# One fused kernel of a mixed transformer block: two in-order queues of the paired attention loop are re-ordered, and the multiplies of the MLA up-projection move from GpSimd to VectorE

## The chip, the cores and the metric

The kernel runs on one core of one Trainium2 chip. The metric is the device time of one execution in microseconds (us). It was run three times; the middle value counts. A core has TensorE (PE; its weight loads are listed as PEld), VectorE (DVE), ScalarE (ACT), GpSimd (POOL) and SyncE (SP), each with an in-order queue of its own, joined by semaphores. Work goes through SBUF (tiles named AR, RW, RX, RA) and the eight banks of PSUM (PS).

## The reference, cut to what matters

The reference is a first block (modulation, recurrent mixer, dilated attention) and two further blocks with mixture-of-experts layers. The first of the two, the "even" layer, has a differential attention and a grouped-query attention. The second, the "odd" layer, is a latent attention (MLA) with 16 heads, 512 queries and 768 keys:

```python
def mla_project(h, w_in, q_norm, w_q_up, kv_norm, w_kv_up, qk_norm):
    cq, ckv, kr = jnp.split(h @ w_in, [MLA_Q_RANK, MLA_Q_RANK + MLA_KV_RANK], axis=-1)
    q = (rmsnorm(cq, q_norm) @ w_q_up).reshape(bsz, t, MLA_HEADS, MLA_NOPE + MLA_ROPE)
    kv = (rmsnorm(ckv, kv_norm) @ w_kv_up).reshape(bsz, t, MLA_HEADS, MLA_NOPE + MLA_VDIM)
    qn = rmsnorm(q[..., :MLA_NOPE], qk_norm[0, :MLA_NOPE])
    qr = rmsnorm(q[..., MLA_NOPE:], qk_norm[0, MLA_NOPE:])
    kn = rmsnorm(kv[..., :MLA_NOPE], qk_norm[1, :MLA_NOPE])
    ...
def mla_attend(qn, qr, kn, kr, v, scale):
    s = jnp.einsum('bqhd,bkhd->bhqk', qn, kn) + jnp.einsum('bqhr,bkr->bhqk', qr, kr)
    p = jax.nn.softmax(s.astype(jnp.float32) * scale, axis=-1).astype(v.dtype)
    return jnp.einsum('bhqk,bkhd->bqhd', p, v)
```

## The kernel before

Everything is float32. Each engine's queue is written out by one function per stage, and every engine runs its stages in the same order.

**Paired attention.** Two stages use the `..._pairs` functions: the grouped-query attention of the even layer (ATB, 48 units) and the MLA attention of the odd layer (ATO, 64 units). A unit is 128 queries of one head against 768 keys (256 in the last 16 units of ATB). The loop is a software pipeline over steps. In step s TensorE computes the scores of unit s (line 655) into banks 0 and 1 or 2 and 3, then the fill items of this step, then the transposes of the probabilities of unit s-2 (line 666, into banks 4 and 5; for odd units one more transpose, line 670, of the reciprocal sums), and in even steps the product with the values for units s-4 and s-3 together (line 866, "pv", into bank 6). VectorE takes the maximum of the scores (line 755), a reciprocal (906), copies the transposed probabilities of even units out of PSUM (916), and scales the product out of bank 6 (924, "the scaling"). ScalarE does the exponential (710, two records: the activation and the reading of its sum) and the copy of the odd units (890). GpSimd spreads the reciprocals (834).

**Fill items.** A unit can carry extra work, done four steps later by each engine, as `fill(it)`. In ATO these are the up-projections of the next four heads ("group"): 13 items i = 0 to 12 for each of three groups, one a step; item i stands in step 18+i for the second of them (first item in an even step), item 12 is the last. Group 1 has its items 0 to 2 together in step 4, and then one a step. The very first group is projected ahead of the loop, alone (the "prologue"). A group has ten tiles k, six of key and value (k = 0 to 5) and four of query (k = 6 to 9). Item i does on TensorE the transposes of tile i-3 (line 2500, "ut", into bank 6) and then the projection of tile i (2518 for a key tile, 2511 for a query tile, "up", into bank 7). On ScalarE it copies tile i-3 out of bank 6 (2528), copies tile i out of bank 7 and squares it (2539 and 2540, or 2536 and 2537), and does Ln and Exp (2548, 2550) for the norm of tile i-1, after VectorE's part for it. On VectorE it sums the squares of tile i-1 (2561, 2563, 2565, 2568) and finishes and applies the norm of tile i-2 (2580 to 2588, 2591). On GpSimd it copies parts of tile i-1 (2602, 2606) and multiplies tile i-2 by gain and rotary tables (2617 to 2629), after which the semaphore `upU` lets TensorE transpose it.

A bank is filled again only when its reader is done: "pv" and "ut" share bank 6, so an ut waits for the scaling of the product before it, and a product waits for ScalarE's 2528; "up" of item i+1 waits for ScalarE's square of item i. In ATB the 13 fill items are a square on ScalarE (1785) and a sum on VectorE (1793) for each of six tiles, one norm, and six multiplies (1803), in steps 4 to 16.

The weights of the experts of the odd layer are loaded only after the last product of ATO (`Q.wait_ge("full", "pv", "o", 63)`), and the loads behind ATB wait for its last product in the same way.

Of the kernel before, what the change touches and what calls it, by code (L numbers as in the profile page):

```python
# [6 lines left out]
ALU = mybir.AluOpType  # L7
# [127 lines left out]
class Banks:  # L135
# [5 lines left out]
    def fill(self, b, *label):  # L141
        n = self.n.get(b, 0)
        if n and self.e.seen.get(f"read{b}", 0) < n:
            self.e.e.wait_ge(self.c.sem(f"read{b}"), n)
            self.e.seen[f"read{b}"] = n
        self.n[b] = n + 1
        self.c.bank[label] = (b, n + 1)
        return b
# [5 lines left out]
def program(nc, T, out, known):  # L154
    ctx = ExitStack()
    with ctx:
# [19 lines left out]
        def bank(b):  # L176
            return PS[:, b, :]
# [700 lines left out]
        def act_pairs(A, fill=None):  # L878
            n = len(A.units)
            for step in range(n + 4):  # L880
                i = step - 4
                if 0 <= i < n:
                    for it in A.fill[i]:
                        fill(it)
                i = step - 2
                if i % 2 and 0 <= i < n:
                    nk = A.units[i]["nk"] + 128
                    pt_free(S, A, i)
                    S.wait_ge("full", "tr", A.tag, i)
                    s.copy(A.Pt[i % len(A.Pt)][:, 0:nk], psf[:, 2048:2048 + nk]).then_inc(*S.read("tr", A.tag, i))  # L890
                if step < n:
                    act_exp(A, step)

        def dve_pairs(A, fill=None):
            n = len(A.units)
            for step in range(n + 4):
                if step < n:
                    dve_max(A, step)
                i = step - 1
                if i % 2 and 0 <= i < n:  # L900
                    a = (i - 1) % 8
                    V.wait_ge("read", "sc", A.tag, i - 1)
                    V.wait_ge("read", "sc", A.tag, i)
                    if i >= 8:
                        V.wait_ge("rb", A.tag, i - 8)
                    v.reciprocal(A.rd[:, a:a + 2], A.den[:, a:a + 2]).then_inc(*V.up("rd", A.tag, i))
                i = step - 4
                if 0 <= i < n:
                    for it in A.fill[i]:
                        fill(it)  # L910
                i = step - 2
                if i % 2 == 0 and 0 <= i < n:
                    nk = A.units[i]["nk"]
                    pt_free(V, A, i)
                    V.wait_ge("full", "tr", A.tag, i)
                    v.tensor_copy(A.Pt[i % len(A.Pt)][:, 0:nk], psf[:, 2048:2048 + nk])\
                        .then_inc(*V.read("tr", A.tag, i))
                i = step - 3
                if i % 2 and 0 <= i < n:
                    b = V.bank_of(("pv", A.tag, i))  # L920
                    nk = A.units[i]["nk"]
                    V.wait_ge("read", "tr", A.tag, i)
                    V.wait_ge("full", "pv", A.tag, i)
                    v.tensor_tensor(A.units[i]["out"], bank(b)[:, 0:128], A.Pt[i % len(A.Pt)][:, nk:nk + 128], ALU.mult)\
                        .then_inc(*V.read("pv", A.tag, i))


        OUTP = {"oute": 6, "outo": 4}
# [1624 lines left out]
        def dve_up(gi, i):  # L2553
            if 0 <= i - 1 < 10:
                k = i - 1
                isq = UP[k][1]
                A_, U_, W_, q_ = STM[(10 * gi + k) % 3]
                n_, hw_ = (8, 96) if isq else (4, 64)
                Sv = U_[:, 0:4 * hw_].rearrange("p (h f) -> p h f", h=4)
                V.wait_ge("read", "up", gi, k)  # L2560
                v.tensor_reduce(q_[:, 0:4], Sv[:, :, 0:64], AX, ALU.add).then_inc(*V.up("upr", gi, k))
                if isq:
                    v.tensor_reduce(q_[:, 4:8], Sv[:, :, 64:96], AX, ALU.add).then_inc(*V.up("upw"))
                    V.wait_ge("upw")
                    v.tensor_scalar(q_[:, 4:8], q_[:, 4:8], 2.0, None, ALU.mult).then_inc(*V.up("upw"))
                    V.wait_ge("upw")
                V.wait_ge("upr", gi, k)
                v.tensor_scalar(q_[:, 8:8 + n_], q_[:, 0:n_], 1.0 / 64, EPS, ALU.mult, ALU.add)\
                    .then_inc(*V.up("upa", gi, k))
            if 0 <= i - 2 < 10:  # L2570
                k = i - 2
                j, isq = UP[k]
                A_, U_, W_, q_ = STM[(10 * gi + k) % 3]
                n_ = 8 if isq else 4
                a_, y_, z_ = q_[:, 8:8 + n_], q_[:, 8 + n_:8 + 2 * n_], q_[:, 0:n_]
                Av = (A_[:, 0:384] if isq else A_).rearrange("p (h f) -> p h f", h=4)
                Uv = U_.rearrange("p (h f) -> p h f", h=4)
                Wv = W_.rearrange("p (h f) -> p h f", h=4)
                V.wait_ge("upy", gi, k)
                v.tensor_tensor(z_, y_, y_, ALU.mult).then_inc(*V.up("upw"))  # L2580
                V.wait_ge("upw")
                v.tensor_tensor(z_, z_, a_, ALU.mult).then_inc(*V.up("upw"))
                V.wait_ge("upw")
                v.tensor_scalar(z_, z_, -0.5, 1.5, ALU.mult, ALU.add).then_inc(*V.up("upw"))
                V.wait_ge("upw")
                v.tensor_tensor(y_, y_, z_, ALU.mult).then_inc(*V.up("upw"))
                V.wait_ge("upw")
                v.tensor_tensor(Av[:, :, 0:64], Av[:, :, 0:64], y_[:, 0:4].unsqueeze(2).broadcast_to([128, 4, 64]),
                                ALU.mult).then_inc(*V.up("upn", gi, k))
                if isq:  # L2590
                    v.tensor_tensor(Av[:, :, 64:96], Av[:, :, 64:96],
                                    y_[:, 4:8].unsqueeze(2).broadcast_to([128, 4, 32]), ALU.mult)\
                        .then_inc(*V.up("upw", gi, k))

        def pool_up(gi, i):
            k = i - 1
            if 0 <= k < 10 and not UP[k][1]:
                j = UP[k][0]
                A_, U_, W_, q_ = STM[(10 * gi + k) % 3]
                grp_free(G, gi)  # L2600
                G.wait_ge("read", "up", gi, k)
                g.tensor_copy(GRP[gi % 2][2][:, j, :].rearrange("p (h f) -> p h f", h=4),
                              A_.rearrange("p (h f) -> p h f", h=4)[:, :, 64:128]).then_inc(*G.up("upv", gi, j))
                G.wait_ge("kr", 5)
                G.wait_ge("upr", gi, k)
                g.tensor_copy(U_.rearrange("p (h f) -> p h f", h=4)[:, :, 64:96],
                              krn[:, j, :].unsqueeze(1).broadcast_to([128, 4, 32])).then_inc(*G.up("upk", gi, k))
            k = i - 2
            if 0 <= k < 10:
                j, isq = UP[k]  # L2610
                A_, U_, W_, q_ = STM[(10 * gi + k) % 3]
                Av = (A_[:, 0:384] if isq else A_).rearrange("p (h f) -> p h f", h=4)
                Uv = U_.rearrange("p (h f) -> p h f", h=4)
                Wv = W_.rearrange("p (h f) -> p h f", h=4)
                gg = gm[:, 0:64] if isq else gm[:, 96:160]
                G.wait_ge("upn", gi, k)
                t = g.tensor_tensor(Uv[:, :, 0:64], Av[:, :, 0:64], gg.unsqueeze(1).broadcast_to([128, 4, 64]), ALU.mult)
                if isq:
                    G.wait_ge("upw", gi, k)
                    g.tensor_tensor(Uv[:, :, 64:96], Av[:, :, 64:96],  # L2620
                                    TM[:, 0, j, 0, :].unsqueeze(1).broadcast_to([128, 4, 32]), ALU.mult)
                    for q4 in range(4):
                        p4 = q4 ^ 1
                        t = g.tensor_tensor(Wv[:, :, 8 * q4:8 * q4 + 8], Av[:, :, 64 + 8 * p4:72 + 8 * p4],
                                            TM[:, 0, j, 1, 8 * q4:8 * q4 + 8].unsqueeze(1).broadcast_to([128, 4, 8]),
                                            ALU.mult)
                    t.then_inc(*G.up("upr4", gi, k))
                    G.wait_ge("upr4", gi, k)
                    t = g.tensor_tensor(Uv[:, :, 64:96], Uv[:, :, 64:96], Wv, ALU.add)
                t.then_inc(*G.up("upU", gi, k))  # L2630

        OT4 = AR[:, XN0:XN0 + 4096].rearrange("p (c t) -> p c t", c=8)
        units, fills = [], {}
# [233 lines left out]
```

## Time and profile before

| what | value |
|---|---|
| time, median of 3 runs | 2594.24 us (2591.68 to 2594.48) |
| the profiled execution | 2594.48 us |
| its span in the trace | 2593.2 us |
| busy in the span | PE 2268.0 us (87%), PEld 1280.5 (49%), DVE 1288.5 (50%), ACT 985.4 (38%), POOL 463.1 (18%) |
| ATB, paired part | about 745 to 857 us |
| up-projection ahead of ATO (prologue) | about 1681 to 1721 us |
| ATO | about 1721 to 1977 us |

Times in rows are microseconds from the start of the span unless marked ns. PE busy is a modelled figure, since matmuls are pipelined; a granted clock (PEclk) of 1.00 is 2.4 GHz and 0.50 is 1.2 GHz.

### The profile page before, as it was taken

The page shows a single profiled execution, that of the slowest core. Times are in us where ns is not written, and L with a number is a line of the kernel's source. Part 1 is how long each engine was busy: PE and PEld are TensorE (multiplying, and loading weights), DVE is VectorE, ACT ScalarE, POOL GpSimd, SP SyncE. Part 2 cuts the span into 40 slices and gives each one's busy share as a digit, 9 for nine tenths or more (in the row PEclk, how much of TensorE's full clock was granted, in tenths as well). Part 3 has the DMA queues.
Part 4 walks back from the last instruction along what each step waited for, and adds up shares of the span by engine and source line. Part 5 has one row for each costly group of instructions (what it writes and reads, how often), then busy time and mean ns, then how long its engine had stood idle before and what let it go on. Part 6 is the DMA issues. An engine that isn't in the chain of part 4 may idle for free.

```text
span 2593.2 us, 26567 instructions
## 1 busy us (share of the span) xinstructions
PE 2268.0 (87%) x10249; PEld 1280.5 (49%) x10249; DVE 1288.5 (50%) x2295; ACT 985.4 (38%) x1612; POOL 463.1 (18%) x463
## 2 busy tenths in 40 slices
PE   5998988999989995999999997779999887777776
PEld 2443534445657453667666674436665432222222
DVE  2137524625875226898889985456662421111111
ACT  2015333213554124888888884245552100000000
POOL 0000000000111111354456620032321000000000
PEclk8999989999999997999999998889999889999999
DMA  7111511011000337899999998300014689999998
GB/s 271 65 65 66 197 63 69 33 49 66 1 1 1 131 155 276 334 370 367 381 372 370 369 364 297 125 1 1 1 66 163 252 316 404 403 401 403 404 412 342
DMA packets 92428, 546.32 MB, mean 211 GB/s; under 512 B 7791, under 2 KB 10623, under 8 KB 67598
## 3 DMA queue, kind: packets, MB, share of 16 engines
q1 hardware_dynamic: 81886, 518.95, 51.0%
q0 software_dynamic: 6144, 20.98, 3.6%
q10 hardware_dynamic: 4272, 4.69, 0.5%
q8 instruction: 82, 1.34, 0.2%
q14 instruction: 44, 0.36, 0.0%
HBM read 523.62 MB, written 20.97 MB: 210 GB/s over the span
## 4 chain that ended last, share of the span: by engine, by line
PE 53%; DMA 17%; DVE 16%; ACT 7%; issue 5%; POOL 1%; SPq 0%; ACTq 0%; DVEq 0%; POOLq 0%
DMA AR<-in_w_exp_gate_dram 13%; PE PS L655 7%; PE PS L1650 7%; DVE RW L1996 7%; PE PS L953 5%; PE PS L2030 5%; PE PS L2215 4%; PE PS L666 3%; PE PS L866 3%; ACT AR L2084 3%; PE PS L1340 3%; ACT RW L1988 2%; PE PS L1174 2%; PE PS L415 2%; PE PS L690 2%
## 5 line engine op out<-in xcount | busy, mean ns | idle before, releaser
L2215 PE MATMUL PS<-AR 128*64 128x512 f32 x1536 | 371.6, 631 | 99.1 <-DMA AR<-in_w_exp_gate_dram 48.7
L1996 DVE TENSOR_TENSOR RW<-AR,RW 128x2048 fp32r<-128x2048 f32 x192 | 432.2, 2283 | 51.1 <-ACT RW L1988 51.1
L1988 ACT CAST RW<-AR 128x2048 fp32r<-128x2048 f32 x192 | 364.1, 1913 | 119.3 <-PE PS L2030 111.6
L2030 PE MATMUL PS<-RW,RX 128*96 128x512 f32 x1536 | 364.3, 396 | 9.9 <-DVE RX L2129 9.4
L2030 PEld LDWEIGHTS PS<-RW,RX 128*96 128x96 f32 x1536 | 248.5, 163 | 116.6 <-issue 10.6
L2215 PEld LDWEIGHTS PS<-AR 128*64 128x64 f32 x1536 | 113.8, 144 | 332.9 <-issue 261.6
L655 PE MATMUL PS<-AR 128*128 128x256 f32 (+5 forms) x640 | 243.7, 498 | 4.2 <-POOL AR L640 2.3
L1650 PE MATMUL PS<-AR 128*128 128x512 f32 (+1 forms) x480 | 193.0, 559 | 5.2 <-DMA AR<-in_w_in_even_dram 5.2
L2030 PE MATMUL PS<-RW,RA 128*96 128x512 f32 x768 | 185.6, 398 | 11.6 <-DVE RA L2163 11.6
L755 DVE TENSOR_REDUCE AR<-PS 128x1 f32<-128x768 f32 (+1 forms) x160 | 135.9, 849 | 114.9 <-PE PS L655 114.5
L2279 POOL DMA_INDIRECT AR<-h_rows,AR x32 | 164.1, 5127 | 112.2 <-DVE AR L1965 48.7
L2292 POOL DMA_INDIRECT x_rows<-AR x16 | 119.3, 7456 | 328.8 <-DVE AR L2173 268.2
L2232 ACT COPY AR<-PS 128x512 f32<-128x512 f32 x16 | 9.4, 586 | 410.3 <-PE PS L2200 410.3
L655 PEld LDWEIGHTS PS<-AR 128*128 128x128 f32 (+1 forms) x640 | 110.2, 195 | 100.8 <-issue 94.9
L2030 PEld LDWEIGHTS PS<-RW,RA 128*96 128x96 f32 x768 | 123.2, 164 | 68.4 <-issue 18.4
L710 ACT ACTIVATE AR<-PS,AR 128x768 f32<-128x768 f32 (+1 forms) x160 | 130.5, 816 | 59.6 <-DVE AR L760 25.5
L640 POOL COPY AR<-AR 64x128 f32<-64x128 f32 x80 | 25.3, 322 | 702.4 <-ACT AR L1690 311.9
L953 PE MATMUL PS<-AR 128*128 128x512 f32 x320 | 137.8, 593 | 1.1 <-DVE AR L976 0.6
L1650 PEld LDWEIGHTS PS<-AR 128*128 128x128 f32 x480 | 91.1, 193 | 94.7 <-issue 92.5
L666 PE MATMUL PS<-AR 128*128 128x128 f32 x800 | 118.0, 277 | 18.8 <-ACT AR L732 7.5
L666 PEld LDWEIGHTS PS<-AR 128*128 128x128 f32 x800 | 94.3, 142 | 59.0 <-issue 15.9
L1340 PE MATMUL PS<-AR 128*128 128x512 f32 x256 | 111.8, 592 | 0.0
(332 smaller groups left out, 2641.3 us busy)
## 6 DMA issues: line engine op xcount, KB each, us to landing
AR<-in_w_exp_gate_dram SPq DMA_DIRECT2D x64, 2048.0 KB, 13.2
AR<-in_w_exp_up_dram SPq DMA_DIRECT2D x64, 2048.0 KB, 11.0
AR<-in_w_exp_down_dram SPq DMA_DIRECT2D x64, 2048.0 KB, 22.7
AR<-in_w_ada_dram SPq DMA_DIRECT2D x30, 2048.0 KB, 9.4
AR<-in_w_in_dram SPq DMA_DIRECT2D x6, 2048.0 KB, 7.9
AR<-in_w_in_even_dram SPq DMA_DIRECT2D x4, 2048.0 KB, 8.5
AR<-in_w_out_dram SPq DMA_DIRECT2D x2, 2048.0 KB, 8.7
AR<-in_w_out_even_dram SPq DMA_DIRECT2D x2, 2048.0 KB, 7.8
```

What stands on the lines that cost most here:

```text
L655: m = pe.matmul(PS[:, p0 + a // 512, 0:e_ - a], q, u["k"][:, a:e_], start=True, stop=True)
L666: m = pe.transpose(PS[:, 4 + k // 4, 128 * (k % 4):128 * (k % 4) + 128], pc[:, 128 * k:128 * k + 128], ident)
L710: ex = s.activation(pc[:, 0:nk], pc[:, 0:nk] if A.masked else psf[:, 512 * p0:512 * p0 + nk], ACT.Exp, bias=A.mx[:, i % 8:i % 8 + 1], accu ...
L755: v.tensor_reduce(nm, sc_, AX, ALU.max, negate=True).then_inc(*V.up("mx", A.tag, i))
L953: m = pe.matmul(bank(b), OT[:, c, 128 * j:128 * j + 128], w[:, c, :], start=(c == 0), stop=(c == 7))
L1340: m = pe.matmul(bank(b), HT4[:, k, 128 * j:128 * j + 128], w[:, k, :], start=(k == 0), stop=(k == 7))
L1650: m = pe.matmul(bank(b)[:, 0:a1 - a0], HT6[:, k, 128 * j:128 * j + 128], w[:, k, :], start=(k == 0), stop=(k == 7))
L1988: s.copy(pair(i)[0], raw_half(key, hf)).then_inc(*S.up("hi", l, i))
L1996: v.tensor_tensor(lo, raw_half(key, hf), hi.bitcast(F32), ALU.subtract).then_inc(*V.up("split", key, hf))
L2030: m = pe.matmul(bank(ob)[0:Mc, :], st_, mv[:, k, 512 * q_:512 * q_ + 512], start=(k0 + k == 0 and n_ == 0), stop=(k0 + k == 7 and n_ == 2))
L2215: m = pe.matmul(bank(b)[64 * q_:64 * q_ + 64, :], op, w[:, c, 512 * q_:512 * q_ + 512], start=(h == 0 and c == 0), stop=(h == 1 and c == 3 ...
L2279: g.indirect_dma_start(xs[e % 3], None, T["h_rows"], bass.IndirectOffsetOnAxis(ap=IDX[0:R, e:e + 1], axis=0))\
```

## The change

In ScalarE's paired loop the fill items move from the front of a step to its end, behind the copy and the exponential. In VectorE's paired loop the scaling of the product moves from the end of step s to the front of step s+1, ahead of the maximum; the fill items move from the middle (behind the reciprocal) to the end of the step, behind the copy of the transposed probabilities. TensorE's and GpSimd's loops keep their order. In the up-projection, the multiplies by gain and rotary tables move from GpSimd (`pool_up`) to VectorE (`dve_up`), directly behind the norm of the same tile, with the same operations on the same tiles.

```diff
         def act_pairs(A, fill=None):
             for step in range(n + 4):
-                i = step - 4
-                if 0 <= i < n:
-                    for it in A.fill[i]:
-                        fill(it)
                 i = step - 2
                 if i % 2 and 0 <= i < n:
...
                 if step < n:
                     act_exp(A, step)
+                i = step - 4
+                if 0 <= i < n:
+                    for it in A.fill[i]:
+                        fill(it)
 
         def dve_pairs(A, fill=None):
             for step in range(n + 4):
+                i = step - 4
+                if i % 2 and 0 <= i < n:
...
+                    v.tensor_tensor(A.units[i]["out"], bank(b)[:, 0:128], A.Pt[i % len(A.Pt)][:, nk:nk + 128], ALU.mult)\
+                        .then_inc(*V.read("pv", A.tag, i))
                 if step < n:
                     dve_max(A, step)
...
-                i = step - 4
-                if 0 <= i < n:
-                    for it in A.fill[i]:
-                        fill(it)
                 i = step - 2
                 if i % 2 == 0 and 0 <= i < n:
...
-                i = step - 3
-                if i % 2 and 0 <= i < n:
...
-                    v.tensor_tensor(A.units[i]["out"], bank(b)[:, 0:128], A.Pt[i % len(A.Pt)][:, nk:nk + 128], ALU.mult)\
-                        .then_inc(*V.read("pv", A.tag, i))
+                i = step - 4
+                if 0 <= i < n:
+                    for it in A.fill[i]:
+                        fill(it)
...
         def dve_up(gi, i):
...
+                V.wait_ge("upn", gi, k)
+                gg = gm[:, 0:64] if isq else gm[:, 96:160]
+                t = v.tensor_tensor(Uv[:, :, 0:64], Av[:, :, 0:64], gg.unsqueeze(1).broadcast_to([128, 4, 64]), ALU.mult)
+                if isq:
+                    V.wait_ge("upw")
+                    v.tensor_tensor(Uv[:, :, 64:96], Av[:, :, 64:96],
+                                    TM[:, 0, j, 0, :].unsqueeze(1).broadcast_to([128, 4, 32]), ALU.mult)
+                    for q4 in range(4):
+                        p4 = q4 ^ 1
+                        t = v.tensor_tensor(Wv[:, :, 8 * q4:8 * q4 + 8], Av[:, :, 64 + 8 * p4:72 + 8 * p4],
+                                            TM[:, 0, j, 1, 8 * q4:8 * q4 + 8].unsqueeze(1).broadcast_to([128, 4, 8]),
+                                            ALU.mult)
+                    t.then_inc(*V.up("upw"))
+                    V.wait_ge("upw")
+                    t = v.tensor_tensor(Uv[:, :, 64:96], Uv[:, :, 64:96], Wv, ALU.add)
+                t.then_inc(*V.up("upU", gi, k))
...
         def pool_up(gi, i):
...
-            k = i - 2
-            if 0 <= k < 10:
...
-                G.wait_ge("upn", gi, k)
-                t = g.tensor_tensor(Uv[:, :, 0:64], Av[:, :, 0:64], gg.unsqueeze(1).broadcast_to([128, 4, 64]), ALU.mult)
...
-                    t = g.tensor_tensor(Uv[:, :, 64:96], Uv[:, :, 64:96], Wv, ALU.add)
-                t.then_inc(*G.up("upU", gi, k))
```

## Rows read from the trace of the kernel before

**Rows 1.** Chain of work that ended last, 1640 to 2000, by line.
```profile
by line: PE PS L655 23.1%; PE PS L866 13.7%; PE PS L666 10.7%; PE PS L2403 6.5%; PE PS L953 6.5%; PE PS L2518 6.3%; PE PS L2500 5.2%; PE PS L2511 4.5%; issue 3.1%; POOL AR L2624 2.2%; POOL AR L2617 2.0%; DVE AR L755 1.9%; POOL AR L2629 1.2%
```
**Rows 2.** Stretches between products: length, busy per engine, PEclk, DMA share, GB/s.
```profile
core 0: us, PE busy (x) PEld busy (x) DVE busy (x) ACT busy (x) POOL busy (x), PEclk, DMA share, GB/s
1680.30:1719.00 38.70, 21.68 (x64) 9.59 (x64) 20.87 (x84) 16.88 (x49) 17.80 (x45) 0.75 0.00 0
...
1784.81:1792.17 7.36, 7.36 (x47) 5.45 (x49) 2.82 (x4) 2.64 (x5) 0.00 (x0) 0.77 0.01 2
...
1806.07:1814.80 8.73, 8.43 (x60) 5.59 (x61) 7.04 (x24) 6.09 (x16) 3.24 (x8) 1.00 0.02 4
...
1823.96:1833.42 9.46, 9.30 (x64) 6.36 (x65) 6.56 (x23) 6.02 (x16) 1.69 (x3) 1.00 0.01 2
1833.42:1843.45 10.03, 8.18 (x59) 5.49 (x58) 7.42 (x27) 5.53 (x15) 5.11 (x15) 1.00 0.00 0
1843.45:1852.62 9.17, 6.96 (x54) 4.85 (x54) 4.87 (x13) 4.17 (x10) 5.33 (x16) 1.00 0.01 2
...
1926.06:1931.72 5.66, 5.66 (x47) 4.10 (x49) 3.13 (x6) 2.79 (x5) 0.30 (x1) 1.00 0.01 3
```
**Rows 3.** Timeline, one odd step of group 2: start, length, instruction, idle before.
```profile
1807.46 1.56 PE L655 MATMUL PS<-AR 96*128 96x512 f32 x4
...
1808.86 0.60 PE L2500 MATMUL PS<-AR 128*96 128x128 f32 x4
...
1809.30 1.02 PE L2518 MATMUL PS<-AR 128*128 128x512 f32 x2
1809.50 0.58 ACT L2528 COPY AR<-PS 96x512 f32<-96x512 f32 x1 [1.94 <-PE PS L2500]
...
1809.93 0.41 DVE L2561 TENSOR_REDUCE AR<-AR 128x4 f32<-128x256 f32 x1
...
1810.16 0.82 PE L666 MATMUL PS<-AR 128*128 128x128 f32 x6
...
1810.36 0.59 ACT L2539 COPY AR<-PS 128x512 f32<-128x512 f32 x1 [0.28 <-PE PS L2518]
...
1810.84 0.39 ACT L2540 ACTIVATE AR<-PS 128x256 f32<-128x256 f32 x1
...
1811.35 0.42 DVE L2588 TENSOR_TENSOR AR<-AR 128x256 f32<-128x256 f32 x1
...
1811.47 0.89 ACT L890 COPY AR<-PS 128x896 f32<-128x896 f32 x1
...
1812.25 0.91 ACT L710 ACTIVATE AR<-PS,AR 128x768 f32<-128x768 f32 x1
```
**Rows 4.** Waits, 1700 to 2000: in total, times, longest.
```profile
PE PS L2500 <- POOL AR L2629: 21.1, 13, 4.2
```
**Rows 5.** Groups by form, 1719 to 1977 and 600 to 2000: busy, mean ns.
```profile
L2617 POOL TENSOR_TENSOR AR<-AR 128x256 f32<-128x256 f32 x30 | 21.8, 728 | 62.0 <-DVE AR L2588 62.0
...
L2624 POOL TENSOR_TENSOR AR<-AR 128x32 f32<-128x32 f32 x48 | 10.5, 251 | 0.0
...
L916 DVE COPY AR<-PS 128x768 f32<-128x768 f32 x32 | 30.3, 947 | 9.3 <-PE PS L666 9.0
...
L924 DVE TENSOR_TENSOR AR<-PS,AR 128x128 f32<-128x128 f32 x32 | 9.3, 291 | 16.1 <-PE PS L866 16.0
...
L1611 DVE TENSOR_TENSOR AR<-AR 128x32 f32<-128x32 f32 x16 | 2.0, 183 | 0.0
```
**Rows 6.** Timeline of ATB, step 6: the fill item's two instructions.
```profile
757.04 0.63 ACT L1785 ACTIVATE AR<-AR 128x512 f32<-128x512 f32 x1
...
757.70 0.69 DVE L1793 TENSOR_REDUCE AR<-AR 128x4 f32<-128x512 f32 x1
```
**Rows 7.** Timeline of the prologue's last tiles, VectorE and GpSimd.
```profile
1714.33 0.72 POOL L2617 TENSOR_TENSOR AR<-AR 128x256 f32<-128x256 f32 x1 [2.54 <-DVE AR L2588]
1714.37 0.70 DVE L2580 TENSOR_TENSOR AR<-AR 128x8 f32<-128x8 f32 x1
...
1719.02 0.45 POOL L2629 TENSOR_TENSOR AR<-AR 128x128 f32<-128x128 f32 x1
```

More of the change, by code:

```diff
@@ L896, in dve_pairs @@
             for step in range(n + 4):
+                i = step - 4
+                if i % 2 and 0 <= i < n:
+                    b = V.bank_of(("pv", A.tag, i))
+                    nk = A.units[i]["nk"]
+                    V.wait_ge("read", "tr", A.tag, i)
+                    V.wait_ge("full", "pv", A.tag, i)
+                    v.tensor_tensor(A.units[i]["out"], bank(b)[:, 0:128], A.Pt[i % len(A.Pt)][:, nk:nk + 128], ALU.mult)\
+                        .then_inc(*V.read("pv", A.tag, i))
                 if step < n:
@@ L917, in dve_pairs @@
                         .then_inc(*V.read("tr", A.tag, i))
-                i = step - 3
-                if i % 2 and 0 <= i < n:
[L920 to L923, printed above, removed]
-                    v.tensor_tensor(A.units[i]["out"], bank(b)[:, 0:128], A.Pt[i % len(A.Pt)][:, nk:nk + 128], ALU.mult)\
-                        .then_inc(*V.read("pv", A.tag, i))
+                i = step - 4
+                if 0 <= i < n:
+                    for it in A.fill[i]:
+                        fill(it)
         OUTP = {"oute": 6, "outo": 4}
@@ L2591, in dve_up @@
                     v.tensor_tensor(Av[:, :, 64:96], Av[:, :, 64:96],
-                                    y_[:, 4:8].unsqueeze(2).broadcast_to([128, 4, 32]), ALU.mult)\
-                        .then_inc(*V.up("upw", gi, k))
+                                    y_[:, 4:8].unsqueeze(2).broadcast_to([128, 4, 32]), ALU.mult).then_inc(*V.up("upw"))
+                V.wait_ge("upn", gi, k)
[14 more added lines that the diff above has]
+                t.then_inc(*V.up("upU", gi, k))
         def pool_up(gi, i):
@@ L2607, in pool_up @@
                               krn[:, j, :].unsqueeze(1).broadcast_to([128, 4, 32])).then_inc(*G.up("upk", gi, k))
-            k = i - 2
-            if 0 <= k < 10:
[L2610 to L2615, printed above, removed]
-                G.wait_ge("upn", gi, k)
-                t = g.tensor_tensor(Uv[:, :, 0:64], Av[:, :, 0:64], gg.unsqueeze(1).broadcast_to([128, 4, 64]), ALU.mult)
[L2618 to L2628, printed above, removed]
-                    t = g.tensor_tensor(Uv[:, :, 64:96], Uv[:, :, 64:96], Wv, ALU.add)
-                t.then_inc(*G.up("upU", gi, k))
         OT4 = AR[:, XN0:XN0 + 4096].rearrange("p (c t) -> p c t", c=8)
```

## The prediction

> **What bounds the kernel now.** I read the page first for the shares: TensorE is busy 87% of the span. Then the chain of work for 1640 to 2000, where the changed code does most [rows 1]: it is nearly all TensorE's, with GpSimd's multiplies (L2617, L2624, L2629) as the largest foreign part, 5.4% of 360 us or 19 us, part of it in the prologue. Then the paired loop cut into stretches from one product to the next, two steps each [rows 2]. A pair without fill items takes 5.66 us and TensorE is busy for all of it. A pair with two key items takes 8.73, of which 8.43 busy; one with query items 9.46 of 9.30. So these are set by TensorE. Only the last two pairs of a group's items (10.03 and 9.17 us) leave it idle, 1.85 and 2.21 us: there it waits for GpSimd's last multiply [rows 4], 21.1 us in all, prologue included. This wait is what a faster route to `upU` can give back; all else can only be kept or lost. ATB's full pairs are built like the unfilled ones. Time lost in either loop is not regained later, because the loads behind each wait for its last product.
>
> **The change, part by part.**
>
> *The multiplies on VectorE.* The first of them has the shape of L2588, which VectorE does in 0.42 us [rows 3] against 0.73 on GpSimd [rows 5]. A key tile has this one alone. A query tile adds a 128x128 multiply, four of 128x32 and a 128x128 add; by L924's 0.29 for 128x128 and 0.18 for 128x32 [rows 5] that is 0.42+0.29+4x0.18+0.29 = 1.7 us, and as unwaited instructions overlap by up to 0.1 each I take 1.4. Bounds: 1.2 if the small ones overlap by half, and 2.5, which is what GpSimd took for the same set (0.73 to the start of L2629 at its end [rows 5, 7]). VectorE's own item cost 1.84 us for a key tile (1809.93 to the end of L2588, 1811.77 [rows 3]); a query tile sums and scales a second part of 128x128, by L924's 0.29 twice and less overlap 0.5 more, 2.35. It becomes 2.3 and 3.7.
>
> *A rule that speaks for the move.* An unshared small multiply on VectorE takes 0.16 us, but one took 0.70 beside GpSimd's multiply [rows 7]. The Trainium skill (SBUF — State Buffer, Who interferes with whom) says that a VectorE instruction with two SBUF inputs contends with GpSimd's reads; the trace agrees. By this alone VectorE would gain some 0.1 us an item, and the sum would be about 3 us lower.
>
> *The orders.* Follow one pair of group 2 in the new order. Time 0 is the start of ut in an odd step. Up follows at 0.44, the transposes at 1.30, and ScalarE can begin its copy at 2.25 (1808.86 to 1811.1, the end of L670's work behind L666 [rows 3]). The copy takes 0.78 to the start of the exponential, and this with its reading 1.07 [rows 3]. Only then come L2528, L2539 and L2540, about 1.35 together: they end at 5.45. Before, ScalarE did them ahead of its copy, at 1809.50 to 1811.2, while TensorE was still transposing. They now gate TensorE: the up of the even step needs bank 7 and starts at 5.5, not 3.8 (scores, 1.40, and ut stand before it in either). Its transposes start at 6.36 and are done at 7.2. VectorE's copy takes 0.95 [rows 5] to 8.15, the fill item behind it 2.3 to 10.45, and the scaling, which now stands behind that item, to 10.8. The next odd step's ut needs both `upU` from this item and bank 6 from the scaling, so it starts at 10.85. The pair goes round in 10.85 us, not 8.73. Nothing of it overlaps, for each engine's queue holds the next engine's need behind work of its own.
>
> The same sum for the other pairs of a group: with a query up in the even step 11.25 (0.43 more); with two query ups and the query multiplies 5.95+0.05 (ScalarE's part, after an up of 1.29) +1.29+0.86+0.95+3.7+0.35 = 13.2; the next, without an up in the even step, 0.5+5.1+0.86+1.0+3.7+0.35 = 11.5; and from the last odd ut to the scores of step 31 7.8 us, through ScalarE's copy, exponential, L2528 twice and the product of 1.46. On the way in, with 0 at the up of step 19, its transposes end and ScalarE's copy starts at 1.8, the square ends at 1.8+0.78+1.07+1.0 = 4.65, and the up of step 20 waits for it where it would start at 0.86+0.76+1.3 = 2.9: 1.75 late. The first ut (step 21, now at 1808.86 [rows 3]) would then be at 1810.6 and waits 0.8 more for `upU` and the scaling: 1811.4. Summed: 1811.4+10.85+11.25+13.2+11.5+7.8 = 1866.0. The kernel before starts the same scores (of step 31) at 1852.62, the start of the product before them [rows 2], plus 1.5: 1854.1. **A group loses 11.9 us, three lose 35.7.** This has already taken back GpSimd's 4 us a group.
>
> With bounds for the query multiplies (1.2 and 2.5) two of the even items move, by -0.2 and +1.1 each: -1 to +7 us over three groups.
>
> *ATB.* There the square stands behind the exponential and the sum behind the square. Round a pair: maximum 0.96, exponential 1.1, square 0.63, sum 0.69 [rows 6], twice, and the scaling: 7.3 us with gaps, against 5.66. TensorE has 2 us in hand (scores of a unit need the exponential of two units before), so of the three pairs with squares and the norm behind them some 3 us come through: stepping the queues through them the product of step 14 comes 3.0 us later, and from there no more is added. **+3**; 0 if the slack holds, 5 if not. The 256-key tail and the pairs without fill keep their length, as their orders only move the scaling, which has a step in hand.
>
> *Prologue.* No attention runs here, so only the multiplies count. For key tiles ut comes 0.36 us earlier in a loop that spans two items, some 1.5 us in all; for the query tiles I take 1 us more off, as VectorE's records slowed beside GpSimd (0.70 for 0.16) go, and GpSimd's 2.5 behind the last norm, which end at 1719.47 [rows 7], shrink to 1.4. **-2.5**, from -5 to +2 (VectorE at GpSimd's prices).
>
> *Clock.* Where TensorE's busy share is 0.56, in the prologue, its granted clock is 0.75; after the two pairs at 0.82 and 0.76 the next fell to 0.77 in one group, and 7.36 us stand where 5.7 would [rows 2]. The new pairs hold 8.43 of 10.85 (0.78) and 9.3 of 13.2 (0.70) for longer, so I expect more such stretches at 1.2 GHz: two more a group at 1 to 1.6 us. **+6**, from 0 to +20.
>
> Sum: 35.7+3-2.5+6 = +42 on the profiled execution's 2594.48 (0.2 above the median of the runs), **2637 us**, 1.6% slower.
>
> **The rivals.**
>
> *GpSimd's wait goes and the orders cost nothing: faster.* For it: 4.05 us of idle TensorE a group, with 1.4 us of multiplies in place of 2.5; and the maximum and exponential no longer stand behind a fill item. The Trainium skill (GPSIMD Engine Reference, Engine selection) has elementwise work on VectorE and not on GpSimd, which would make it so. Worked out from the stretches: 3x4.05+2.5 = 14.7 off, 2580 us. It decides if ScalarE's square of an odd step is done before TensorE's next up, 3.8 us after ut; I find 5.45. Against it: pairs are TensorE's by 97% today, so earlier exponentials buy nothing. Chance 0.07.
>
> *Only VectorE's load counts: no change.* If ScalarE's lateness is absorbed, VectorE's work a pair is 3.2 (two maxima, reciprocal, copy, scaling) and two items: 7.8 for key tiles, under 8.73; 10.6 for query tiles, over 9.46 by 1.2, while the two idle pairs shrink by 1 to 2. About 0 a group: 2596. Against it the same two waits. Chance 0.05.
>
> *The clock stays down.* If TensorE sits at 1.2 GHz for half of the three groups' 170 us, its 8.4 us a pair becomes 16.8 in those, more than the loop: some 5 us for each of eight pairs on top, 2670. For it the prologue's 0.75; against it two pairs at 0.8 held 1.00. Chance 0.10.
>
> **How the numbers follow.** The forecast has 0.78. Its own range is 2616 to 2654: the smallest sum is 35.7-8 (if my overlaps of queues are each half too pessimistic) -5+0+0 = +22, the largest 35.7+7+5-1+13 = +60. Between the forecast and the two rivals below lies nothing likely, above it the clock's. 2612 to 2664 leaves out less than 2 in 10. A difference under 0.2% (5 us) can't be told from none here: faster 0.07, same 0.05, slower 0.88.
>
> **What would show it.** Pairs of ATO with fill items at 10.5 to 13.5 us, while pairs without stay at 5.66; idle time of L2518 and L2511 put down to ScalarE's L2540 and L2537, and of L2500 to VectorE's new multiply or the scaling, none to GpSimd; ScalarE's L2528 behind L710 in each step. ATB's first pairs longer by 3 us in all; the prologue shorter. Wrong would be: fill pairs still at 8.7, which would mean the up of the even step isn't held by the square; or the loss all in stretches with a low granted clock.

## The result, and the profile after

The changed kernel takes 2627.25 us (median of 4 runs, 2625.23 to 2629.54) against 2594.36 (2591.68 to 2598.77). The ratio is 1.0126, 95% interval 1.0108 to 1.0143: **slower by 1.3%, 33 us**. 2637 us (2612 to 2664) was forecast. The profiled execution took 2626.1 us with a span of 2624.8, 31.6 more than the span before.

Cutting both traces at the same instructions shows where. ATB is taken from the last line-690 product to the first line-939 transpose, the prologue from the first line-2518 matmul to the first scores of ATO, and ATO from there to the first matmul of the out-projection behind it:

| stage | before | after | difference |
|---|---|---|---|
| up to ATB | 739.8 | 741.7 | +1.9 |
| ATB | 117.9 | 120.2 | +2.3 |
| between, unchanged code | 823.7 | 823.9 | +0.2 |
| prologue | 40.0 | 36.7 | -3.3 |
| ATO | 255.5 | 288.9 | +33.4 |
| behind ATO | 616.3 | 613.4 | -2.9 |

Stages whose code nobody touched differ by up to about 3 us between two executions. ATB's difference is plain all the same: in the kernel before and in the experiments below that leave ATB's loops alone or change only VectorE's order there, it took 117.5 to 118.0 us. Nearly all of the loss is ATO's. The stretches of ATO after the change (columns as in [rows 2]; the first row is the prologue):

```profile
1685.84:1722.49 36.65, 21.90 (x68) 10.19 (x69) 25.79 (x116) 17.57 (x50) 4.18 (x12) 0.80 0.00 0
1819.78:1830.72 10.94, 8.92 (x58) 5.51 (x57) 7.26 (x21) 5.49 (x16) 1.57 (x5) 1.00 0.01 1
1842.11:1853.76 11.65, 9.79 (x62) 6.28 (x61) 7.36 (x23) 5.92 (x16) 0.83 (x3) 1.00 0.01 2
1853.76:1866.25 12.49, 8.31 (x59) 5.56 (x58) 10.61 (x41) 5.43 (x14) 0.30 (x1) 1.00 0.00 0
1866.25:1875.85 9.60, 7.02 (x54) 4.85 (x54) 8.33 (x35) 4.14 (x9) 0.30 (x1) 1.00 0.01 2
1875.85:1881.50 5.65, 5.65 (x45) 4.10 (x45) 2.06 (x4) 1.77 (x3) 0.00 (x0) 1.00 0.00 0
```

Against [rows 2], the key pair has grown from 8.73 to 10.94, the query pairs from 9.46, 10.03 and 9.17 to 11.65, 12.49 and 9.60, and the pair without items has kept its length. TensorE's busy time has grown by 0.1 to 0.5 us in each, so what was added is nearly all idle time. No engine is full: VectorE works 7.3 of 10.94 us, and 10.6 of 12.49 in its busiest pair. The timeline of one key pair shows where the time lies (start, length, instruction, idle before it and what ended that):

```profile
1823.57 0.64 PE L2500 MATMUL PS<-AR 128*96 128x128 f32 x4 [0.77 <-DVE AR L903]
...
1824.05 1.02 PE L2518 MATMUL PS<-AR 128*128 128x512 f32 x2
...
1824.91 0.82 PE L666 MATMUL PS<-AR 128*128 128x128 f32 x6
...
1825.93 0.91 ACT L886 COPY AR<-PS 128x896 f32<-128x896 f32 x1 [4.01 <-PE PS L670]
...
1826.73 0.91 ACT L710 ACTIVATE AR<-PS,AR 128x768 f32<-128x768 f32 x1
...
1827.62 0.57 ACT L2528 COPY AR<-PS 96x512 f32<-96x512 f32 x1
...
1828.25 0.64 PE L2500 MATMUL PS<-AR 128*96 128x128 f32 x4 [1.12 <-ACT AR L2528]
1828.56 0.40 ACT L2540 ACTIVATE AR<-PS 128x256 f32<-128x256 f32 x1
...
1829.01 1.12 PE L2518 MATMUL PS<-AR 128*128 128x512 f32 x2
...
1830.90 0.96 DVE L920 COPY AR<-PS 128x768 f32<-128x768 f32 x1 [2.70 <-PE PS L666]
...
1831.78 0.41 DVE L2561 TENSOR_REDUCE AR<-AR 128x4 f32<-128x256 f32 x1
...
1833.84 0.42 DVE L2595 TENSOR_TENSOR AR<-AR 128x256 f32<-128x256 f32 x1
1834.18 0.28 DVE L903 TENSOR_TENSOR AR<-PS,AR 128x128 f32<-128x128 f32 x1
...
1834.52 0.39 PEld L2500 LDWEIGHTS PS<-AR 128*96 128x96 f32 x4 [1.18 <-DVE AR L903]
```

Read it as one chain: ut of the odd step at 1823.57, up, transposes, ScalarE's copy (886, once 890) and exponential, and only then ScalarE's copy of ut (2528, started at 1809.50 in [rows 3], 0.64 us after its ut; here 4.05 after) and its square, which ends at 1828.96. The even step's up starts at 1829.01, 5.44 us after ut. Then transposes, VectorE's copy (920, once 916), its whole item with the moved multiply (2595), the scaling (903, once 924), and the next odd step's ut at 1834.52. It goes round in 10.95 us. The waits of 1700 to 2020 say the same (us in total, times, longest). TensorE waited for GpSimd's L2629 for 21.1 us before [rows 4]; now no wait for it is left, and these stand in its place:

```profile
PEld PS L2500 <- ACT AR L2528: 26.3, 17, 2.0
...
PEld PS L2500 <- DVE AR L903: 20.8, 15, 2.3
PE PS L2500 <- ACT AR L2528: 16.8, 15, 1.1
PE PS L2500 <- DVE AR L903: 14.8, 15, 1.9
...
PEld PS L2518 <- ACT AR L2540: 9.4, 7, 2.8
...
PE PS L2500 <- DVE AR L2607: 7.8, 4, 2.9
```

A wait of the weight load (PEld) and of the matmul behind it are the same idle time seen twice, so the rows of PEld and PE are not to be added.

### The profile page after: what moved, and what is told of

The parts are those of the page before. It is cut to its first block, busy times and chain, and to the rows that moved or that the text cites. A ratio compares the mean times of both kernels' runs of the same rounds, so it can differ in the third digit from the quotient of the medians.

```text
span 2624.8 us, 26582 instructions
## 1 busy us (share of the span) xinstructions
PE 2271.9 (87%) x10249; PEld 1279.2 (49%) x10249; DVE 1315.0 (50%) x2431; ACT 984.0 (37%) x1612; POOL 398.2 (15%) x327
## 4 chain that ended last, share of the span: by engine, by line
PE 50%; DMA 18%; DVE 18%; ACT 9%; issue 5%; SPq 0%; ACTq 0%; POOL 0%; DVEq 0%; POOLq 0%
DMA AR<-in_w_exp_gate_dram 13%; PE PS L1650 7%; DVE RW L1996 7%; PE PS L655 6%; PE PS L953 5%; PE PS L2215 4%; PE PS L2030 4%; PE PS L666 3%; ACT AR L2084 3%; PE PS L1340 3%; ACT RW L1988 2%; PE PS L1174 2%; PE PS L866 2%; PE PS L415 2%; PE PS L690 2%
## 5 line engine op out<-in xcount | busy, mean ns | idle before, releaser
L1988 ACT CAST RW<-AR 128x2048 fp32r<-128x2048 f32 x192 | 364.1, 1913 | 118.0 <-PE PS L2030 110.3
L2030 PEld LDWEIGHTS PS<-RW,RX 128*96 128x96 f32 x1536 | 247.8, 162 | 116.0 <-issue 10.6
L2279 POOL DMA_INDIRECT AR<-h_rows,AR x32 | 154.3, 4821 | 110.8 <-DVE AR L1965 48.7
## 6 DMA issues: line engine op xcount, KB each, us to landing
AR<-in_w_exp_up_dram SPq DMA_DIRECT2D x64, 2048.0 KB, 11.5
```

The source lines that it names most:

```text
L1988: s.copy(pair(i)[0], raw_half(key, hf)).then_inc(*S.up("hi", l, i))
L2030: m = pe.matmul(bank(ob)[0:Mc, :], st_, mv[:, k, 512 * q_:512 * q_ + 512], start=(k0 + k == 0 and n_ == 0), stop=(k0 + k == 7 and n_ == 2))
L2279: g.indirect_dma_start(xs[e % 3], None, T["h_rows"], bass.IndirectOffsetOnAxis(ap=IDX[0:R, e:e + 1], axis=0))\
```

## The experiments

The change has three parts that can be taken alone: ScalarE's order, VectorE's order, and the multiplies on VectorE. All combinations were run, then four kernels aimed at single instructions. Each was timed in 5 rounds beside the kernel before on the same chip; the ratios are to the kernel before of the same rounds (medians 2594.64 to 2596.02), so they are the better measure of small differences. Theory: the two orders close the chain above, and the multiplies by themselves help. First rival: VectorE's load is what costs. Second rival: only one of the orders matters.

| kernel | median us | ratio to before, 95% interval | ATB | prologue | ATO |
|---|---|---|---|---|---|
| before | 2594.36 | 1 | 117.9 | 40.0 | 255.5 |
| ScalarE's order alone | 2626.97 | 1.0121 (1.0106 to 1.0136) | 129.1 | 39.4 | 280.2 |
| VectorE's order alone | 2613.32 | 1.0066 (1.0051 to 1.0080) | 117.5 | 40.1 | 275.0 |
| multiplies alone | 2582.95 | 0.9951 (0.9935 to 0.9967) | 118.0 | 36.0 | 248.4 |
| both orders | 2637.32 | 1.0154 (1.0136 to 1.0172) | 119.7 | 41.8 | 295.8 |
| VectorE's order, multiplies | 2600.06 | 1.0017 (1.0008 to 1.0026) | 118.0 | 36.7 | 262.8 |
| ScalarE's order, multiplies | 2619.26 | 1.0088 (1.0074 to 1.0102) | 127.7 | 36.6 | 272.1 |
| all three (the change) | 2627.25 | 1.0126 (1.0108 to 1.0143) | 120.2 | 36.7 | 288.9 |

### ScalarE's order alone

```diff
 (act_pairs alone as in the change)
-                for it in A.fill[i]: fill(it)      # ahead of the copy
                 ... copy, act_exp(A, step)
+                for it in A.fill[i]: fill(it)      # behind the exponential
```

> The kernel before with ScalarE's new order alone (fill items behind copy and exponential); VectorE's order and GpSimd's multiplies stay. Loop theory (each engine's queue holds the next one's need): the up of the even step still waits for ScalarE's square at 5.45 us after ut, but VectorE's item stands ahead of its copy, so from there on the pair is TensorE's: a key pair takes 10.0 us and not 8.73, a query pair 10.85 and not 9.46, and the pairs that waited for GpSimd stay near 10.0 and 9.2. Some 6 us a group, 1 to 2 in ATB: 2614 us (2608 to 2620). Rival, that only VectorE's place and load count: no change, 2594.

2626.97 us: a loss, and 13 us more than expected (the range ended at 2620). In ATO (+24.7 us, where some 18 were expected) the pairs with key items and the first with query items behave as worked out. The key pairs take 9.97 us, the query pairs 10.83 (TensorE idle until ScalarE's L2528 in each, as here):

```profile
1830.14 0.60 PE L2500 MATMUL PS<-AR 128*96 128x128 f32 x4
...
1834.78 0.64 PE L2500 MATMUL PS<-AR 128*96 128x128 f32 x4 [1.12 <-ACT AR L2528]
1835.54 0.70 PE L2518 MATMUL PS<-AR 128*128 128x512 f32 x1
```

The up follows its ut by 5.40 us, where 5.45 was worked out. What I had undervalued is the last two pairs of a group (10.37 and 11.06, each waiting on ScalarE and GpSimd in turn) and ATB, 11.2 us longer instead of 1 to 2. There VectorE's sum waits for ScalarE's square, and its copy out of PSUM is queued behind that sum, so TensorE waits for the copy; at 766.2 its clock has fallen too (granted 0.56 from 766.2 to 770.0; the six transposes, 0.82 us at 760.06, take 1.52):

```profile
763.85 0.62 ACT L1785 ACTIVATE AR<-AR 128x512 f32<-128x512 f32 x1
764.50 0.69 DVE L1793 TENSOR_REDUCE AR<-AR 128x4 f32<-128x512 f32 x1 [1.50 <-ACT AR L1785]
765.10 0.95 DVE L916 COPY AR<-PS 128x768 f32<-128x768 f32 x1
...
766.20 1.52 PE L666 MATMUL PS<-AR 128*128 128x128 f32 x6 [2.37 <-DVE AR L916]
```

With VectorE's new order its copy goes ahead of the sum, and ATB is back at 119.7 to 120.2. So in ATB the second re-ordering mends most of what the first breaks. A part of this kernel's loss is the clock: from 1738.9 to 2012.6 the mean granted clock is 0.96, where the kernel before has 0.99 from 1726.9 to 1976.9.

### VectorE's order alone

```diff
 (dve_pairs alone as in the change: copy, fill items, then scaling, maximum)
```

> The kernel before with VectorE's new order alone (fill items behind its copy, scaling behind them); ScalarE's order and GpSimd's multiplies stay. Loop theory: the up of the even step starts at 3.95 us after ut as before, VectorE's copy ends at 6.6, its item at 8.45, GpSimd's multiply at 9.25, ut at 9.3: a key pair takes 9.3 us, a query pair up to 12.0 since GpSimd's 2.6 us now lie behind it. Some 6 us a group, 1 to 2 in ATB: 2614 us (2608 to 2622). Rival, that ScalarE's place alone costs: no change, 2594.

2613.32 us, as expected, with key pairs of 9.2 us and the two late query pairs of a group at 11.2 to 14.0, since GpSimd's 2.6 us now lie behind a later item. ATB kept its length, where 1 to 2 us were expected. Here too some of the loss is the clock, at a mean of 0.94 from 1729.4 to 1999.0; at 1850.52 four matmuls of L2511 take 2.77 us that took 1.46 in a full-clock stretch of the changed kernel (1859.17). Neither order is harmless alone; the second rival falls.

### The multiplies alone

```diff
 (dve_up and pool_up alone as in the change)
```

> The kernel before with the multiplies on VectorE alone, both orders as before. Loop theory: key pairs stay at 8.73 us, pairs with two query items are bound by VectorE (3.2 plus 7.4 = 10.6 us, not 9.46), the pairs that waited for GpSimd shrink from 10.0 and 9.2 to about 9.6 and 7.2, the prologue by 3.4 as in the changed kernel: 2588 us (2582 to 2593), faster than before. Rival, that VectorE's load is what made the changed kernel slow: slower than 2600.

2582.95 us, the fastest kernel of this study and 0.5% faster than before. The first rival falls: VectorE's load is not what made the change slow. The late pairs of a group fall from 10.1 and 9.2 to 9.2 and 9.0, and the prologue takes 36.0. The gain is about twice what I expected, and the expectation was wrong in two places that nearly cancel: the pair that I had as bound by VectorE at 10.6 us takes 9.12, and the last pair of a group, which I had at 7.2, takes 9.0. What is left comes in small parts from the key pairs (8.6 and 9.0 for 8.73 and 9.16) and the prologue, and 3.2 us of it from the clock: the kernel before has two stretches at 1.2 GHz inside ATO, and this profile has none there behind 1724.6. VectorE is indeed full for a while (no gaps from 1825.6 to 1842). A round of it with two such items takes 9.95 us (1825.64 to 1835.59), not 10.6; that the rest of its lateness is taken up by slack between the queues is my reading, which no run isolates. Its item with all multiplies takes 3.55 us, from here to the start of the copy behind it:

```profile
1825.64 0.42 DVE L2561 TENSOR_REDUCE AR<-AR 128x4 f32<-128x256 f32 x1 [0.22 <-issue]
...
1827.92 0.42 DVE L2595 TENSOR_TENSOR AR<-AR 128x256 f32<-128x256 f32 x1
1828.26 0.28 DVE L2598 TENSOR_TENSOR AR<-AR 128x128 f32<-128x128 f32 x1
1828.46 0.49 DVE L2602 TENSOR_TENSOR AR<-AR 128x32 f32<-128x32 f32 x4
1828.98 0.29 DVE L2607 TENSOR_TENSOR AR<-AR 128x128 f32<-128x128 f32 x1
1829.19 0.95 DVE L916 COPY AR<-PS 128x768 f32<-128x768 f32 x1
```

### Both orders, the multiplies on GpSimd

```diff
 (act_pairs and dve_pairs as in the change, dve_up and pool_up as before)
```

> The kernel before with both new orders, the multiplies left on GpSimd. Loop theory: key pairs as in the changed kernel (10.9 us), query pairs longer by what GpSimd takes more than VectorE (2.65 against 1.35 us, twice a group), the prologue as before (3.4 longer): 2638 us (2632 to 2645), slower than the changed kernel's 2627. Rival, VectorE's load: faster than the changed kernel, 2615 or less.

2637.32 us, 10 more than the change and as expected: in the profiles 6.9 more in ATO and 5.1 in the prologue (3.4 expected). Moving the multiplies back on top of the two orders is a loss, never a gain.

### The change without ScalarE's order, and without VectorE's

```diff
 (e5: act_pairs as before)
 (e6: dve_pairs as before)
```

> The changed kernel with ScalarE's old order put back (VectorE's new order and the multiplies on VectorE stay). Loop theory: the up of the even step is free of the square again, so key pairs take 9.25 us and not 10.95, the query pairs about 11, ATO some 265 us, ATB 117.5 as with VectorE's order alone, the prologue 36.5: 2602 us (2597 to 2608). Rival, that the two orders add and the multiplies are neutral: 2613.

> The changed kernel with VectorE's old order put back (ScalarE's new order and the multiplies on VectorE stay). Loop theory: key pairs 10.0 us, query pairs about 10.8, the pairs behind GpSimd's wait near 10, ATO some 273 us; ATB 129 as with ScalarE's order alone; prologue 36.5: 2618 us (2612 to 2624).

2600.06 and 2619.26 us. The key pairs are 9.24 and 9.97 us, worked out as 9.25 and 10.0. So in the change ScalarE's order costs 27 us (2627.25 against 2600.06) and VectorE's 8 (against 2619.26); from the other end, with the multiplies alone as the start, they cost 36 and 17, and 44 together. They overlap by 9 us. In the profiles 7.5 us of overlap are ATB's mending above. In ATO it is the other way round: 24 and 14 us apart, 40.5 together, so there the two orders cost more together than apart. The rest lies in code that no part touches: the kernel without ScalarE's order spends 827.2 us between ATB and the prologue, with a granted clock of 0.50 from 859.0 to 872.7, where the kernel with the multiplies alone spends 823.

### Only the norm late, not the copies

```diff
 (kernel before; act_up split)
+        def act_up_late(gi, i):          # Ln and Exp of tile i-1, the same instructions
...
 (act_pairs, ATO alone)
                 fill(it)                  # in front: copies out of banks 6 and 7, square
                 ... copy, act_exp(A, step)
+                late(it)                  # behind: Ln and Exp
```

> The kernel before with ScalarE's items of the up-projection split: the copies out of banks 6 and 7 and the square stay in front of copy and exponential, Ln and Exp alone go behind the exponential. If it is the copies and the square behind the exponential that cost (ScalarE's order alone made ATO 280 us), ATO stays at 255.5 or falls by up to 3: 2595 us (2590 to 2598). If Ln and Exp arriving late is what costs, ATO is near 280: 2620.

> The same split with the multiplies on VectorE, VectorE's order as before: a candidate for the fastest. The exponential no longer waits for VectorE's part of the norm, so VectorE's full stretches delay less: ATO 246 to 249 us against 248.4 with the multiplies alone, 2581 us (2576 to 2586). Rival, Ln and Exp late delay VectorE's next item: slower than 2590.

Without the multiplies on VectorE it takes 2597.88 us (ratio 1.0011, 1.0002 to 1.0021), with them 2585.66 (0.9955, 0.9942 to 0.9969), the same as the multiplies alone. In the profile of the second the key pairs take 8.58, the query pairs 9.12. The profile of the first has 259.4 us in ATO, 3.9 more than before and above what I expected, mostly in the last two pairs of group 1 (10.98 and 10.80). A late Ln and Exp cost little (0.1%) and give nothing; the fastest kernel that I had hoped for in the second did not come.

### The change with ScalarE's copies and square back in front

```diff
 (the changed kernel; act_pairs with fill in front and late behind, as above)
```

> The changed kernel with only ScalarE's copies out of banks 6 and 7 and its square put back in front of copy and exponential; Ln and Exp stay behind the exponential, VectorE as changed. If these copies and nothing else of ScalarE's new order hold TensorE, this equals the changed kernel with all of ScalarE's old order (2600.1 measured): 2600 us (2596 to 2605), key pairs 9.25 us and ATO 263. If the place of Ln and Exp counts too, it stays above 2610.

2600.74 us (1.0023, 1.0013 to 1.0032), which equals the 2600.06 without any of ScalarE's new order. In ATO (262.4 us) all that ScalarE's order costs is then in the place of its copies out of banks 6 and 7 and the square; which of the three was not separated. In ATB this kernel has all of ScalarE's fill items in front again (118.0 us), so it says nothing on single instructions there.

### One multiply back on GpSimd

```diff
 (the kernel with the multiplies alone)
-                t = v.tensor_tensor(Uv[:, :, 0:64], Av[:, :, 0:64], gg..., ALU.mult)     # key and query tiles
+                if not isq: t = v.tensor_tensor(Uv[:, :, 0:64], ...)                     # key tiles alone
+                g.tensor_tensor(U_...[:, :, 0:64], A_...[:, :, 0:64], gm[:, 0:64]..., ALU.mult)  # pool_up, query tiles
+                P.wait_ge("upG", gi, k)                                                 # pe_up
```

> The kernel with the multiplies on VectorE and both old orders (2583 measured), but the first 128x256 multiply of the query tiles back on GpSimd, beside VectorE's rotary ones. VectorE's query item shrinks by 0.34 us, GpSimd's 0.73 ends before VectorE's 1.1 of rotary work, so `upU` comes earlier in the pairs that VectorE fills: 2581 us (2577 to 2586). Rival, contention on two-input multiplies and a second wait for TensorE eat it: 2584 or more.

2587.74 us (0.9970, 0.9958 to 0.9982): no gain, as the rival had it. It is 5 us slower than with all of them on VectorE (0.9951, 0.9935 to 0.9967). These intervals overlap a little, so the sign rests on the profiles too: ATO takes 251.0 against 248.4 us, and the last pair of a group 9.53 against 9.0. VectorE's item is one multiply of 0.34 us shorter on paper and longer on the chip, 3.86 us from 1827.24 to 1831.10, as the first rotary multiply starts 0.39 us behind the instruction ahead of it, not 0.20, and beside GpSimd's takes 0.65 instead of 0.28 (so do eleven of ATO's twelve):

```profile
1829.32 0.28 DVE L2593 TENSOR_TENSOR AR<-AR 128x128 f32<-128x128 f32 x1
1829.49 0.72 POOL L2630 TENSOR_TENSOR AR<-AR 128x256 f32<-128x256 f32 x1 [11.00 <-DVE AR L2590]
...
1829.71 0.65 DVE L2601 TENSOR_TENSOR AR<-AR 128x128 f32<-128x128 f32 x1
...
1830.28 0.58 DVE L2605 TENSOR_TENSOR AR<-AR 128x32 f32<-128x32 f32 x4
1830.89 0.29 DVE L2610 TENSOR_TENSOR AR<-AR 128x128 f32<-128x128 f32 x1
```

The Trainium skill (SBUF — State Buffer, Who interferes with whom) says that a VectorE instruction with two SBUF inputs contends with a GpSimd instruction that reads SBUF. This run agrees, for 0.37 us on that multiply. Whether TensorE's second wait (`upG`) costs anything beside it was not separated.

## Why the prediction was right

- **What bounds the kernel**: shown. Pairs without items kept 5.66 us in every kernel wherever the granted clock was 1.00, and what moved the time of the others were waits, and the clock in some.
- **The orders, key pair** (10.85 worked out): 10.94 in the trace, with up at 5.44 us after ut (5.45 to 5.5 worked out). The experiments with one order alone have 9.97 and 9.20, where the same sum gave 10.0 and 9.3.
- **The group** (11.9 us, three 35.7): ATO's pairs between the first and the last item of groups 1, 2 and 3 are longer by 11.0, 11.1 and 11.3 in all, 33.4 together. From ut to ut of the odd steps (1823.57, 1834.52, 1845.74, 1858.69, 1869.95) the second group took 10.95, 11.22, 12.95 and 11.26 us, where 10.85, 11.25, 13.2 and 11.5 were worked out; the way out took 7.4, not 7.8. With the clock taken out (below), each of the three groups costs 11.1 us.
- **ATB** (+3): +2.3, for the reason named and with the mending that the sum contained without my seeing it: ScalarE's order alone costs 11.
- **Prologue** (-2.5): -3.3 here, -4.0 with the multiplies alone.
- **The multiplies** (item 3.7 for a query tile): 3.55. The range's upper bound, VectorE at GpSimd's price, was far off.
- **Clock** (+6, up to +20): this is the term that was mis-sized; it came to 0. Behind its first scores ATO has two short stretches at 1.2 GHz in either kernel, not more after than before, and a mean granted clock of 0.98 in both. Before, they made three pairs longer by 1.6, 0.5 and 1.1 us. After, one makes the fourth pair of the third group longer by 1.7 (14.17 against 12.49 of the same pair in the second), and the other falls on the up and the transposes ahead of the first product (2.07 and 1.48 us, where 1.12 and 0.82 stand at full clock), about 1.5. The rows of the kernel after, with the whole pair in the middle, and then those of the kernel before:

```profile
1738.50:1741.90 3.40, 3.21 (x8) 1.81 (x8) 0.00 (x0) 0.14 (x1) 0.00 (x0) 0.50 0.00 0
1934.03:1948.20 14.17, 9.99 (x58) 6.50 (x57) 10.87 (x47) 5.10 (x13) 0.30 (x1) 0.88 0.56 201
1936.50:1939.90 3.40, 3.40 (x10) 2.08 (x9) 3.19 (x17) 0.00 (x0) 0.00 (x0) 0.50 0.02 5
```

```profile
1784.90:1788.30 3.40, 3.40 (x25) 2.77 (x26) 1.25 (x2) 0.75 (x2) 0.00 (x0) 0.50 0.02 5
1918.00:1921.50 3.50, 3.50 (x30) 3.17 (x29) 0.96 (x1) 1.47 (x3) 0.00 (x0) 0.51 0.00 2
```

- **The difference of the sums**: forecast +42.2, measured +31.6 in the profiled execution. Of the 10.6 between them the clock is 6, the three groups 2.3 (35.7 against 33.4), ATB 0.7, the prologue 0.8, and 0.8 lies in code that nobody touched. For the top of the range the prediction summed a clock of +13 and a prologue of -1, though it gave up to +20 and +2 for them; with these the sum comes to +70, which is the 2664 that it states.
- **The rivals**: that GpSimd's wait goes and the orders cost nothing was half right. The wait does go, and with the orders left alone the kernel is 11 to 13 us faster (2582.95); the orders take 44 back. But little of those microseconds is the idle time of 4.05 us a group that the rival counted: the two late pairs shrink by 1.0 us together, since ut then waits for VectorE (in all 5.4 us for its scaling and 4.1 for the last add of its item); 4 us are the prologue's and some 3 the clock's. The rule behind it, elementwise work on VectorE rather than GpSimd (the Trainium skill, GPSIMD Engine Reference, Engine selection), holds for this part. That only VectorE's load counts fell with the multiplies alone. That the clock stays down did not happen here; with one order alone it was down for longer (0.96 and 0.94 above), but never near half of the time.

What is not settled: the 2 us up to ATB and the -3 us behind ATO lie in code that no part touches; they are taken as the spread between executions. The two bounds of ut in the odd step, `upU` and the scaling, were not separated by a run; the trace has the scaling end 0.2 us behind the multiply and release ut. VectorE's new order has two halves, the items behind the copy and the scaling behind the items, and no run takes one without the other.

## What to carry to other kernels

In a pipeline of in-order queues, ask for each instruction that is moved back who waits for it and what of that waiter's work this engine then waits for: a copy that frees a PSUM bank belongs ahead of the long instruction whose input the waiting engine makes, or a chain that was parallel becomes serial, at 2 us a pair here with every engine partly idle. Work such a loop out once around, from the timeline's start times: here the key pair came out within 1% and the whole group within 7%, while a pair worked out from one engine's load alone was 16% off (10.6 against 9.12). And measure the parts of a bundled change alone: this one held a gain of 0.5% beneath a loss of 1.8%.

## What the runs showed of the hardware that was not expected

TensorE's granted clock held 1.00 (2.4 GHz) through pairs of 10 to 12.5 us with a busy share of 0.67 (8.31 of 12.49 us) to 0.84, while the same kernel's prologue, at 0.60 (21.90 of 36.65), had 0.80. But the busy share of a pair does not settle it: the fourth pair of the third group, with the same instructions and the same idle time ahead of its ut as in the second, had a stretch at 1.2 GHz, and in ATB, with ScalarE's order alone, a TensorE idle of 2.4 us stood beside transposes at half speed.

A VectorE multiply of 128x128 with both inputs in SBUF took 0.64 to 0.65 us in fifteen of sixteen cases where a GpSimd multiply of 128x256 had started 0.2 us before it; in the sixteenth, where GpSimd's had started 0.6 us before, it took 0.30, and with none beside it 0.28 us.
